# Seam order and a turned sample product in a two-layer mLSTM / Mamba-2 trunk

## The chip, the cores and the metric

One core of one Trainium2 chip. The metric is device time in microseconds of one execution of the whole program. Engines are named as the profile names them: PE is TensorE, DVE is VectorE, ACT is ScalarE, POOL is GpSimd; SP only issues the weight loads.

## What is computed

One inference step of a decoder trunk with two layers on 256 prompt tokens and 8 samples of 4 tokens each, 288 columns in all. Every layer does `x += mixer(rmsnorm(x))` and `x += convffn(rmsnorm(x))`. Layer 0 mixes with an mLSTM matrix memory, layer 1 with Mamba-2. The part of the Mamba-2 scan that matters here, for each group and head, with `h` the state:

```
cb    = C @ B^T                                   # scores of a group
wts   = cb * exp(-(acum_t - acum_s)) * dt
y     = wts @ x + (C @ h) * exp(acum)             # second term: the state's share
h_new = exp(acum_last) * h + sum(to_end * x * B)
g     = (y + D*x) * silu(z);  g *= rsqrt(mean(g*g) + eps)   # mean over a group of 512
```

For the prompt `h` starts at zero, so the second term exists for the 32 sample columns alone. The channel mixer is `(silu(conv(g)) * conv(v)) @ w_down`, with 2 x 5632 up-projected rows.

## The kernel before

**Layout.** Activations lie turned: features on the 128 partitions, the 288 tokens (`T`; 256 are `TP`, 32 are `TS`) along the free axis. Each matrix product is made in three passes of reduced precision: `w_hi*hi`, `w_hi*lo`, `w_lo*hi` (lines 395 to 397). Weights come in chunks of 128 output rows. For each chunk, in one fixed order through the whole program: SP loads `w_raw`, ACT rounds it to `w_hi` (L672), DVE subtracts to `w_lo` (L999), PE makes 48 products of 288 columns (33 in the down projection, where a chunk has 11 tiles of 128). There are two buffers of each weight tile. A chunk `c` may be split by ACT once PE is through chunk `c-2`. Results go round-robin through four PSUM banks, so PE may run three chunks ahead of DVE. Banks `M0` to `M3` belong to the mixers.

**Order of work.** All queues are written out by hand and in order; semaphores (`wait`, `until`) join them. The mLSTM heads and the Mamba groups are software-pipelined: while PE projects the ten chunks `j = 0..9` of group `u+1`, it does `b_mix(u, p, j)` behind chunk `j`. The steps of a group are: `j = 0` scores and transposes; odd `j` (1, 3, 5, 7) spread the decay rows of head pair `k` over the partitions; even `j` (2, 4, 6, 8) the products of pair `k`; `j = 9` the mean of squares. DVE and ACT do the same steps one place earlier in their loops, with conv and activation of the projected chunk (`b_post`) behind them. POOL holds the transfers of the states: `b_s` (updated and written back) and `b_sT` (the same state turned, only read), 512 KB each, and the weighting `b_xw` (L1651), which ACT and DVE split into `b_x` (L937, L938, L1405) before PE can use it.

**The state's share.** At even `j` PE multiplies the turned state of each of the 8 samples, as 128x128 weights, with 4 columns of `C` (16 instructions, `b_sT`), into `ps[:, M2, T:]`. The factor `exp(acum)` is spread over the partitions at odd `j` by two small products with `b_rsum`. DVE copies it (`b_ea`, L1389), multiplies (`b_yi`, L1412) and adds (L1415). POOL takes the decay of `b_s` from `b_ea` too.

**Seams.** Between stages PE waits for small serial work: the gate rows of either mixer (`gate_columns`, `gate_columns_b`, then `ga_low` / `gb_low`), the sum of squares in front of a channel mixer (`norm(k)` before the first up chunk), and the last `act_lo` between up and down projection. `out_part` opens an output projection with the newest group's tiles last in its order.

Of the kernel before, what the change touches and what calls it, by code (L numbers as in the profile page):

```python
# [25 lines left out]
F32 = mybir.dt.float32  # L26
F32R = mybir.dt.float32r
ACT = mybir.ActivationFunctionType
ALU = mybir.AluOpType
# [93 lines left out]

class Own:
# [17 lines left out]
def trunk(nc, d, o):  # L142

    with ExitStack() as ctx:
# [72 lines left out]
        with ExitStack() as st:  # L217
# [10 lines left out]
            b_yi = sb("b_yi", [P, TS], F32, st)  # L228
            b_rows = sb("b_rows", [64, 3, T], F32, st)
            b_nac2 = sb("b_nac2", [P, T], F32R, st)  # L230
            b_rsum = sb("b_rsum", [64, TS + 1], F32, st)
# [12 lines left out]
            b_ea = sb("b_ea", [P, TS], F32, st)  # L244

# [5 lines left out]
        b_tmp = b_xdt[0:64, 0:2, 0:T]  # L251
        b_th = work[:, :, :].rearrange("p a t -> p (a t)")[:, 0:BP]
# [46 lines left out]
            "b_wts", "b_xwr"))  # L299
        b_yst, b_decayed, b_sadd, b_spr, b_yg, b_gsq, b_gms, b_gvar, b_groot, b_gn, b_ghi, b_glo = map(sem, (  # L300
# [26 lines left out]
        def _(sp):  # L327
# [21 lines left out]
            def ffn(c0, up, down):  # L349
                with sp.Fori(0, 2) as h:  # L350
                    with sp.Fori(0, FH) as i:
                        for j in range(2):
                            load(Count(c0 + j, (h, C_FHALF), (i, 2)), up[h * (2 * FH) + i * 2 + j], CH)
                    with sp.Fori(0, KT) as i:
                        for j in range(2):
                            load(Count(c0 + 2 * FH + j, (h, C_FHALF), (i, 2)), down[h * (2 * KT) + i * 2 + j], DCH)
# [28 lines left out]
        def _(pe):  # L385
# [97 lines left out]
            def a_head(u, p, mixed):  # L483

                c = u.times(6)
                for j in range(6):
# [5 lines left out]
                    if mixed is not None:  # L492
                        a_mix(mixed, 1 - p, j)
# [10 lines left out]
            pe.wait_ge(ga_done, 1)  # L504
            pe.wait_ge(ga_low, 1)
# [28 lines left out]
            def ffn(layer, c0, n0, ea0, ed0, k):  # L534
                norm(k)
                with pe.Fori(0, 2) as h:
                    with pe.Fori(0, FH // 2) as i:
                        for j in range(4):
                            wait(pe, proj_taken, Count(ea0 + j - 3, (h, 2 * FH), (i, 4)))
                            if j == 0:  # L540

                                gemm(Count(c0 + j, (h, C_FHALF), (i, 4)), (n0 + j) % 4, hn_hi, hn_lo, range(KT),
                                     each=lambda t: wait(pe, hn_lo_ready, k * KT + t + 1))
                            else:
                                gemm(Count(c0 + j, (h, C_FHALF), (i, 4)), (n0 + j) % 4, hn_hi, hn_lo, range(KT))
                    wait(pe, f_alo, Count(layer * FT + FH // 2, (h, FH)))
                    pe.sem_inc(pe_passed, 1)
                    with pe.Fori(0, KT // 4) as i:
                        for j in range(4):
                            wait(pe, res_added, Count(ed0 + j - 3, (h, KT), (i, 4)))  # L550
                            for q in range(2):
                                if j == 0 and q == 1:
                                    wait(pe, f_alo, Count(layer * FT + FH, (h, FH)))
                                gemm(Count(c0 + 2 * FH + 2 * j + q, (h, C_FHALF), (i, 8)), (n0 + 2 * FH + j) % 4,
                                     act_hi, act_lo, range(q * FH // 2, (q + 1) * FH // 2), q == 0, q == 1)
# [6 lines left out]
            def gate_columns_b():  # L562
                pe.wait_ge(gb_rows, 1)
                for n, row in enumerate((0, 1, 2)):
                    for b in range(3):
                        w = P if b < 2 else TS
                        m = nc.tensor.transpose(ps[0:w, M1 if n < 2 else M2, 192 * (n % 2) + 64 * b:192 * (n % 2) + 64 * b + 64],
                                                b_rows[:, row, b * P:b * P + w], ident[0:64, 0:64])
                m.then_inc(gb_turned, 1)

            def b_mix(u, p, j):
                bT, cT = b_io[:, p, 0, :], b_io[:, p, 1, :]
                if j == 0:
                    wait(pe, b_silu, u.plus(1).times(6))
                    wait(pe, b_gvar, u)
                    wait(pe, b_sadd, u.times(8))
# [7 lines left out]
                if j in (1, 3, 5, 7):  # L584
# [11 lines left out]
                    mm(ps[:, M1, 0:T], b_sel[:, 1, :], b_nac2[:])  # L596
                    one_head = b_sel[0:64, :, :].bitcast(F32)
                    mm(ps[0:64, M1, T:T + TS], one_head[:, 0, 0:64], b_rsum[:, 0:TS])
                    mm(ps[64:P, M1, T:T + TS], one_head[:, 1, 0:64], b_rsum[:, 0:TS]).then_inc(b_rowsr, 1)
                if j in (2, 4, 6, 8):  # L600
                    k = (j - 2) // 2
                    ch = slice(k * P, (k + 1) * P)
# [3 lines left out]
                    wait(pe, b_sT_in, u.times(4).plus(k + 1).times(16))  # L606
                    for b in range(NB):
                        mm(ps[:, M2, T + SL * b:T + SL * (b + 1)], b_sT[:, b, :], cT[:, TP + SL * b:TP + SL * (b + 1)])
                    for e in range(2):
                        rows, hc = slice(64 * e, 64 * (e + 1)), slice(k * P + 64 * e, k * P + 64 * (e + 1))  # L610
                        mm(ps[rows, M2, 0:TP], b_xdt[:, 0, hc], b_dec[:, e, 0:TP], True, False)
                        mm(ps[rows, M2, P:TP], b_xdt[:, 1, hc], b_dec[:, e, TP:TP + P], False, False)
                        m = mm(ps[rows, M2, TP:T], b_xdt[0:TS, 2, hc], b_dec[0:TS, e, TP + P:SC], False, True)
                    m.then_inc(b_yst, 1)
# [7 lines left out]
                if j == 9:  # L622
                    wait(pe, b_gsq, u.plus(1).times(4))
                    wait(pe, b_yg, u.plus(1).times(4))
                    for k in range(4):
# [1205 lines left out]
```

## Time and profile before

| what | value |
|---|---|
| median of 3 runs | 3375.09 us (3370.61 to 3377.14) |
| the profiled execution's own time | 3377.63 us |
| its span, first to last instruction | 3376.0 us |
| PE busy | 3227.8 us, 96% |
| DVE busy | 2118.9 us, 63% |
| ACT busy | 1351.6 us, 40% |
| POOL busy | 888.1 us, 26% |
| mean granted PE clock | 0.965 |

A busy share is a mean over stages. A row's "idle before" is the time in which the engine did nothing in front of that instruction, with what ended it. PEclk is the mean granted clock of a stretch: 1.0 is 2.4 GHz, 0.5 is 1.2 GHz.

### The profile page before, as it was taken

The page shows a single profiled execution, that of the slowest core. Times are in us where ns is not written, and L with a number is a line of the kernel's source. Part 1 is how long each engine was busy: PE and PEld are TensorE (multiplying, and loading weights), DVE is VectorE, ACT ScalarE, POOL GpSimd, SP SyncE. Part 2 cuts the span into 40 slices and gives each one's busy share as a digit, 9 for nine tenths or more (in the row PEclk, how much of TensorE's full clock was granted, in tenths as well). Part 3 has the DMA queues.
Part 4 walks back from the last instruction along what each step waited for, and adds up shares of the span by engine and source line. Part 5 has one row for each costly group of instructions (what it writes and reads, how often), then busy time and mean ns, then how long its engine had stood idle before and what let it go on. Part 6 is the DMA issues. An engine that isn't in the chain of part 4 may idle for free.

```text
span 3376.0 us, 63895 instructions
## 1 busy us (share of the span) xinstructions
PE 3227.8 (96%) x23321; PEld 3141.6 (93%) x23321; DVE 2118.9 (63%) x3215; ACT 1351.6 (40%) x1694; POOL 888.1 (26%) x1123
## 2 busy tenths in 40 slices
PE   6999999999999999999999999999899999999997
PEld 6999999999999999988888888988799999999997
DVE  5555666666456765567775665676576764466744
ACT  4333334444334444443333333333245443344432
POOL 2110113222012321234541442443232220022221
PEclk9999999999999999999989888998899999999999
DMA  5354444444454444535544444444444444444444
GB/s 203 139 190 174 153 175 153 164 167 143 163 173 169 162 146 162 181 133 186 174 146 160 154 156 158 173 163 154 152 147 161 171 153 153 169 167 165 157 152 143
DMA packets 91383, 545.53 MB, mean 162 GB/s; under 512 B 11688, under 2 KB 12528, under 8 KB 43904
## 3 DMA queue, kind: packets, MB, share of 16 engines
q1 hardware_dynamic: 71872, 466.98, 39.3%
q0 software_dynamic: 19392, 76.98, 6.4%
q8 instruction: 73, 1.20, 0.1%
q14 instruction: 46, 0.38, 0.0%
HBM read 510.92 MB, written 32.99 MB: 161 GB/s over the span
## 4 chain that ended last, share of the span: by engine, by line
PE 79%; DVE 8%; issue 6%; ACT 4%; POOL 2%; DMA 1%; DVEq 0%; POOLq 0%; ACTq 0%; SPq 0%
PE ps L395 25%; PE ps L396 24%; PE ps L397 24%; PE ps L402 6%; ACT w_hi L672 2%; DVE w_lo L999 2%; DVE b_u L1348 1%; POOL sumsq L1506 1%; DVE b_u L1350 1%; DVE b_u L1346 1%; DVE work L1433 0%; DVE sumsq L1428 0%; DVE b_s L1422 0%; POOL b_xw L1651 0%; ACT b_out_hi L953 0%
## 5 line engine op out<-in xcount | busy, mean ns | idle before, releaser
L395 PE MATMUL ps<-hn_hi,w_hi 128*128 128x288 f32 x4896 | 1473.3, 301 | 40.3 <-DVE w_lo L999 17.4
L396 PE MATMUL ps<-hn_lo,w_hi 128*128 128x288 f32 x4896 | 1456.1, 297 | 0.0
L397 PE MATMUL ps<-hn_hi,w_lo 128*128 128x288 f32 x4896 | 1450.6, 296 | 0.0
L999 DVE TENSOR_TENSOR w_lo<-w_raw,w_hi 128x2048 fp32r<-128x2048 f32 (+1 forms) x482 | 1045.2, 2168 | 585.7 <-ACT w_hi L672 585.4
L672 ACT ACTIVATE w_hi<-w_raw 128x2048 fp32r<-128x2048 f32 (+1 forms) x482 | 858.0, 1780 | 1126.9 <-PE ps L397 1120.0
L395 PEld LDWEIGHTS ps<-hn_hi,w_hi 128*128 128x128 f32 x4896 | 930.2, 190 | 46.4 <-issue 24.8
L397 PEld LDWEIGHTS ps<-hn_hi,w_lo 128*128 128x128 f32 x4896 | 933.1, 191 | 0.0
L396 PEld LDWEIGHTS ps<-hn_lo,w_hi 128*128 128x128 f32 x4896 | 931.2, 190 | 1.2
L1583 POOL COPY f_new<-f_pad 128x2 f32 x176 | 242.7, 1379 | 1080.8 <-ACT f_u L847 1080.8
L395 PE MATMUL ps<-act_hi,w_hi 128*128 128x288 f32 x1408 | 416.7, 296 | 13.7 <-DVE act_lo L1278 13.7
L396 PE MATMUL ps<-act_lo,w_hi 128*128 128x288 f32 x1408 | 418.7, 297 | 0.0
L397 PE MATMUL ps<-act_hi,w_lo 128*128 128x288 f32 x1408 | 418.2, 297 | 0.0
L395 PEld LDWEIGHTS ps<-act_hi,w_hi 128*128 128x128 f32 x1408 | 267.9, 190 | 14.6 <-issue 14.6
L396 PEld LDWEIGHTS ps<-act_lo,w_hi 128*128 128x128 f32 x1408 | 267.8, 190 | 0.0
L397 PEld LDWEIGHTS ps<-act_hi,w_lo 128*128 128x128 f32 x1408 | 267.7, 190 | 0.0
L1506 POOL TENSOR_TENSOR sumsq<-sumsq,work 128x288 f32<-128x288 f32 x80 | 121.0, 1513 | 325.7 <-ACT work L687 303.9
L1620 POOL COPY b_new<-b_pad 128x3 f32<-128x3 f32 x48 | 116.6, 2430 | 315.2 <-ACT b_u L904 315.2
L395 PE MATMUL ps<-b_out_hi,w_hi 128*128 128x288 f32 x512 | 159.7, 312 | 23.0 <-DVE b_out_lo L1437 23.0
L850 ACT ACTIVATE act_hi<-f_act 128x288 f32 x88 | 39.1, 445 | 320.7 <-DVE f_act L1275 320.7
L396 PE MATMUL ps<-b_out_lo,w_hi 128*128 128x288 f32 x512 | 156.0, 305 | 0.0
L397 PE MATMUL ps<-b_out_hi,w_lo 128*128 128x288 f32 x512 | 155.7, 304 | 0.0
L395 PEld LDWEIGHTS ps<-b_out_hi,w_hi 128*128 128x128 f32 x512 | 100.9, 197 | 28.5 <-DVE b_out_lo L1437 28.1
(276 smaller groups left out, 3389.1 us busy)
## 6 DMA issues: line engine op xcount, KB each, us to landing
w_raw<-wf_up_in SPq DMA_DIRECT2D x176, 1024.0 KB, 4.8
w_raw<-wf_down_in SPq DMA_DIRECT2D x128, 704.0 KB, 4.0
w_raw<-wb_in_in SPq DMA_DIRECT2D x80, 1024.0 KB, 4.8
w_raw<-wa_in_in SPq DMA_DIRECT2D x48, 1024.0 KB, 5.0
w_raw<-wb_out_in SPq DMA_DIRECT2D x32, 1024.0 KB, 4.8
w_raw<-wa_out_in SPq DMA_DIRECT2D x16, 1024.0 KB, 4.8
b_sT<-b_sT_in POOLq DMA_DIRECT2D x32, 512.0 KB, 5.0
b_s<-b_s_in POOLq DMA_DIRECT2D x32, 512.0 KB, 3.9
```

What stands on the lines that cost most here:

```text
L395: nc.tensor.matmul(out, w_hi[:, s, col], hi[:, t, :], start=first and k == 0, stop=False)
L396: nc.tensor.matmul(out, w_hi[:, s, col], lo[:, t, :], start=False, stop=False)
L397: m = nc.tensor.matmul(out, w_lo[:, s, col], hi[:, t, :], start=False, stop=end)
L402: return nc.tensor.matmul(out, lhs, rhs, start=start, stop=stop, skip_group_check=True)
L672: A(w_hi[:, c.base % 2, 0:cols], w_raw[:, c.base % 2, 0:cols], ACT.Copy).then_inc(w_high, 1)
L850: A(act_hi[:, Count(par).add(i, 2).value, :], f_act[:, par, :], ACT.Copy).then_inc(f_ahi, 1)
L999: TT(w_lo[:, s, 0:cols], w_raw[:, s, 0:cols], w_hi[:, s, 0:cols].bitcast(F32), ALU.subtract).then_inc(w_low, 1)
L1346: STT(out, pad[:, 1:BP - 2], w(1), out, ALU.mult, ALU.add).then_inc(b_taps, 1)
L1348: STT(out, pad[:, 2:BP - 1], w(2), out, ALU.mult, ALU.add).then_inc(b_taps, 1)
L1506: G.tensor_tensor(sumsq[:], sumsq[:], work[:, buf, :], ALU.add).then_inc(sq_added, 1)
L1583: G.tensor_copy(f_new[:, n.value, 0:2], f_pad[:, s, TP:TP + 2])
L1620: G.tensor_copy(b_new[:, j, 0:3], b_pad[:, j % 2, TP:TP + 3])
```

## The change

Four edits of order and one of form, all on the one core:

1. **Gates.** PE's waits for `ga_done`, `ga_low` and for `gb_done`, `gb_low` move behind the first chunk of the second head or group. The gates of layer 1 get two more products, behind the new semaphores `gb_faded` and `gb_spread`.
2. **Channel mixer, start.** PE does the first up chunk tile by tile (`first_project`) and `norm(k)` behind it. ACT and DVE split the next chunk before their part of the norm. POOL loads `f_old` when the mixer is over, not after the norm.
3. **Up to down.** The first four down chunks are taken in the order `FIRST_DOWN`: first halves of two output tiles, then their second halves.
4. **State's share.** `C` of each sample, masked into 32 columns (`b_cm`), is the weight; the turned state streams past it (128 columns), at odd `j`, four samples side by side in four column groups of the array, into `ps[:, M3, P:2P]` (`b_yraw`). ACT takes it out scaled by `exp(acum)` (`b_ysr`), and one product with `fold` adds it to the head pair's sum. `b_ea`, `b_yi` and both adds go; the decay of `b_s` comes from a table `b_fade` made once.
5. **Around it.** The `b_dec` products alternate between the two 64-column halves. The mean of squares takes two products for four; POOL adds tiles 1 and 2 to tile 0 (`b_gsum`). POOL issues the next `b_sT` load at even `j`, in front of `b_xw`, as soon as `b_yraw` says that the buffer was read; before, it was at odd `j` behind the store of `b_s`.

```diff
+FIRST_DOWN = ((0, 0), (1, 0), (0, 1), (1, 1), (2, 0), (2, 1), (3, 0), (3, 1))
# PE, mLSTM: moved from in front of a_head(1) to behind its first chunk
+                        if j == 0 and u.base == 1:
+                            pe.wait_ge(ga_done, 1)
+                            pe.wait_ge(ga_low, 1)
# PE, channel mixer
-                norm(k)
+                        if first and j == 0:
+                            first_project(c, bank, k)
+                            norm(k)
...
+                    down_four(h, 0, FIRST_DOWN)
# PE, gate_columns_b
-                m.then_inc(gb_turned, 1)
+                pe.wait_ge(gb_faded, 1)
+                nc.tensor.transpose(ps[:, M2, 192:256], b_xdt[0:64, 0, 0:P], ident[0:64, 0:64])
+                pe.wait_ge(gb_spread, 1)
+                mm(ps[:, M3, :], mean_mat[0:64, :], b_spread).then_inc(gb_turned, 1)
# PE, b_mix, odd j
-                    mm(ps[0:64, M1, T:T + TS], one_head[:, 0, 0:64], b_rsum[:, 0:TS])
-                    mm(ps[64:P, M1, T:T + TS], one_head[:, 1, 0:64], b_rsum[:, 0:TS]).then_inc(b_rowsr, 1)
+                    wait(pe, b_cmr, u.plus(1))
+                    wait(pe, b_spr, u.times(4).plus(k))
+                    wait(pe, b_sT_in, u.times(4).plus(k + 1).times(16))
+                    for b in range(NB):
+                        g = b % 4
+                        m = mm(ps[TS * g:TS * (g + 1), M3, P:2 * P], b_cm_of[b], b_sT[:, b, :], b < 4, b >= 4)
+                    m.then_inc(b_yraw, 1)
# PE, b_mix, even j
-                    for b in range(NB):
-                        mm(ps[:, M2, T + SL * b:T + SL * (b + 1)], b_sT[:, b, :], cT[:, TP + SL * b:TP + SL * (b + 1)])
+                    wait(pe, b_ysr, u.times(4).plus(k + 1))
+                    for e, (rows, hc) in enumerate(halves):
                         mm(ps[rows, M2, 0:TP], b_xdt[:, 0, hc], b_dec[:, e, 0:TP], True, False)
+                    for e, (rows, hc) in enumerate(halves):
                         mm(ps[rows, M2, P:TP], b_xdt[:, 1, hc], b_dec[:, e, TP:TP + P], False, False)
...
+                    mm(ps[:, M2, TP:T], b_ys, fold[:], False, True).then_inc(b_yst, 1)
# PE, b_mix, j = 9
-                    for k in range(4):
-                        m = mm(ps[:, M2, 0:T], mean_mat[:], b_io[:, p, 2 + k, :], k == 0, k == 3)
+                    mm(ps[:, M2, 0:T], mean_mat[:], b_io[:, p, 2, :], True, False)
                     wait(pe, b_gsq, u.plus(1).times(4))
+                    mm(ps[:, M2, 0:T], mean_mat[:], b_io[:, p, 5, :], False, True).then_inc(b_gms, 1)
# ACT, b_mix, even j, in front of the exponential of b_dec
+                    wait(act, b_yraw, n.plus(1))
+                    for e in range(2):
+                        m = A(b_ys[:, 64 * e:64 * (e + 1)], ps[:, M3, P + 64 * e:P + 64 * (e + 1)], ACT.Copy, scale=b_eas[:, col])
+                    m.then_inc(b_ysr, 1)
# DVE
+                    V.tensor_copy(b_cm[:, :, 0:SL], packed(b_io[:, p, 1, :])).then_inc(b_cmr, 1)
-                    wait(dve, b_decayed, n)
-                    V.tensor_copy(b_ea[:], ps[:, M1, T:T + TS])
-                    b_link(u, 3 * k + 1, TT(b_yi[:], ps[:, M2, T:T + TS], b_ea[:], ALU.mult))
-                    b_link(u, 3 * k + 3, TT(y[:, TP:T], y[:, TP:T], b_yi[:], ALU.add))
+                    dve.wait_ge(gb_faded, 1)
+                    TT(b_spread..., head_ident..., b_ea4..., ALU.mult).then_inc(gb_spread, 1)
# POOL, even j, in front of b_xw
+                    if not (u.base == B_GROUPS - 1 and k == 3):
+                        until(b_yraw, n.plus(1))
+                        load_state(n.plus(1))
# POOL, odd j
-                        load_state(n.plus(1))
+                    if k in (1, 2):
+                        until(b_gsq, n.plus(1))
+                        G.tensor_tensor(b_io[:, p, 2, :], b_io[:, p, 2, :], b_io[:, p, 2 + k, :], ALU.add).then_inc(b_gsum, 1)
```

## Rows read from the trace of the kernel before

**Rows 1.** Waits of TensorE, whole kernel: microseconds in total, times, longest.
```profile
PE ps L402 <- DVE b_dec L1403: 28.3, 14, 5.8
...
PE ps L395 <- DVE act_lo L1278: 13.7, 4, 3.4
```

**Rows 2.** Timeline at the gates of the first mixer: start, length, engine, line, [idle before].
```profile
71.02 2.29 DVE L999 TENSOR_TENSOR w_lo<-w_raw,w_hi 128x2048 fp32r<-128x2048 f32 x1 [1.55 <-ACT w_hi L672]
...
80.76 0.58 PE L395 MATMUL ps<-hn_hi,w_hi 128*128 128x288 f32 x1 [4.99 <-issue]
```

**Rows 3.** Timeline in front of the first channel mixer.
```profile
532.79 2.29 DVE L999 TENSOR_TENSOR w_lo<-w_raw,w_hi 128x2048 fp32r<-128x2048 f32 x1 [1.01 <-ACT w_hi L672]
...
541.39 2.01 DVE L1014 SCALAR_TENSOR_TENSOR hn_lo<-x,norm_w,hn_hi  x2
...
543.14 1.33 PE L402 MATMUL ps<-sumsq,mean_mat 128*128 128x288 f32 x2 [5.94 <-POOL sumsq L1506]
```

**Rows 4.** Timeline between up and down projection, first half of layer 0.
```profile
830.19 2.29 DVE L999 TENSOR_TENSOR w_lo<-w_raw,w_hi 128x2048 fp32r<-128x2048 f32 x1 [1.34 <-ACT w_hi L672]
...
836.55 1.63 DVE L999 TENSOR_TENSOR w_lo<-w_raw,w_hi 128x1408 fp32r<-128x1408 f32 x1 [0.75 <-ACT w_hi L672]
...
835.97 0.40 PE L395 MATMUL ps<-act_hi,w_hi 128*128 128x288 f32 x1 [3.40 <-DVE act_lo L1278]
```

**Rows 5.** Timeline at the gates of the state-space mixer.
```profile
1482.84 0.45 DVE L1322 TENSOR_TENSOR b_nac<-b_rows,b_nac 64x288 fp32r<-64x288 f32 x1
...
1497.38 0.68 DVE L1375 TENSOR_TENSOR b_xdt<-ps,b_dtc 128x512 f32<-128x512 f32 x1
...
1483.39 0.58 PE L395 MATMUL ps<-hn_hi,w_hi 128*128 128x288 f32 x1 [4.80 <-issue]
```

**Rows 6.** Stretches: length, busy time and instructions by engine, PEclk, DMA.
```profile
836.00:842.00 6.00, 6.00 (x34) 6.00 (x35) 1.63 (x1) 0.52 (x1) 0.00 (x0) 0.72 0.40 124
1483.40:1492.00 8.60, 8.60 (x46) 8.60 (x47) 0.00 (x0) 0.00 (x0) 0.00 (x0) 0.68 0.33 121
1583.00:1793.00 210.00, 196.93 (x1338) 182.70 (x1337) 152.32 (x268) 80.92 (x119) 94.38 (x112) 0.92 0.47 162
```

**Rows 7.** TensorE blocks of a mixing step at full clock, and two forms like the new ones.
```profile
104.77 1.07 PE L402 MATMUL ps<-a_c,a_rows 128*32 128x256 f32 x16
...
1733.22 0.30 PE L402 MATMUL ps<-b_rsum,b_sel 64*64 64x32 f32 x4
...
1739.95 1.84 PE L402 MATMUL ps<-b_io,b_sT 128*128 128x4 f32 x16
1741.72 2.11 PE L402 MATMUL ps<-b_dec,b_xdt 128*64 128x256 f32 x12
```

**Rows 8.** Waits of VectorE in two mixing groups, 1583.3 to 1793.7 us.
```profile
DVE b_x L1405 <- ACT b_x L938: 17.8, 8, 3.5
DVE w_lo L999 <- ACT w_hi L672: 11.9, 12, 1.5
...
DVE b_io L1337 <- PE ps L397: 4.5, 3, 2.4
...
DVE b_pad L1334 <- PE ps L397: 1.6, 1, 1.6
```

**Rows 9.** Lines of VectorE and GpSimd: count, busy us, mean ns, idle before.
```profile
L1415 DVE TENSOR_TENSOR b_io<-b_io,b_yi 128x32 f32<-128x32 f32 x32 | 11.6, 362 | 1.1
...
L1412 DVE TENSOR_TENSOR b_yi<-ps,b_ea 128x32 f32<-128x32 f32 x32 | 5.8, 181 | 5.5 <-PE ps L402 5.4
...
L1506 POOL TENSOR_TENSOR sumsq<-sumsq,work 128x288 f32<-128x288 f32 x80 | 121.0, 1513 | 325.7 <-ACT work L687 303.9 <-ACT work L726 16.9 <-POOL sumsq L1506 2.9
...
L1601 POOL DMA_DIRECT2D b_sT<-b_sT_in x32 | 16.9, 529 | 1.8 <-issue 1.6
```

**Rows 10.** TensorE at the end of the last mixing group, half clock.
```profile
2418.89 3.57 PE L402 MATMUL ps<-b_io,b_sT 128*128 128x4 f32 x16 [5.76 <-DVE b_dec L1403]
...
2428.81 4.21 PE L402 MATMUL ps<-b_io,mean_mat 128*128 128x288 f32 x8 [0.70 <-ACT b_io L946]
```

More of the change, by code:

```diff
@@ L534, in ffn @@
             def ffn(layer, c0, n0, ea0, ed0, k):
-                norm(k)
[L536 to L546, printed above, removed]
-                    pe.sem_inc(pe_passed, 1)
[L548 to L555, printed above, removed]
@@ new lines, in up_four @@
+                def up_four(h, i, first=False):
+                    for j in range(4):
+                        wait(pe, proj_taken, Count(ea0 + j - 3).add(h, 2 * FH).add(i, 4))
+                        c, bank = Count(c0 + j).add(h, C_FHALF).add(i, 4), (n0 + j) % 4
+                        if first and j == 0:
+                            first_project(c, bank, k)
+                            norm(k)
+                        else:
+                            gemm(c, bank, hn_hi, hn_lo, range(KT))
@@ new lines, in down_four @@
+                def down_four(h, i, order):
+                    for n, (j, q) in enumerate(order):
+                        if q == 0:
+                            wait(pe, res_added, Count(ed0 + j - 3).add(h, KT).add(i, 4))
+                        elif order is FIRST_DOWN and j == 0:
+                            wait(pe, f_alo, Count(layer * FT + FH).add(h, FH))
+                        gemm(Count(c0 + 2 * FH + n).add(h, C_FHALF).add(i, 8), (n0 + 2 * FH + j) % 4,
+                             act_hi, act_lo, range(q * FH // 2, (q + 1) * FH // 2), q == 0, q == 1)
@@ new lines, in half @@
+                def half(h, done):
+                    with pe.Fori(0, FH // 2 - done) as i:
+                        up_four(h, i if done == 0 else i + done)
+                    wait(pe, f_alo, Count(layer * FT + FH // 2).add(h, FH))
+                    pe.sem_inc(pe_passed, 1)
+                    down_four(h, 0, FIRST_DOWN)
+                    with pe.Fori(0, KT // 4 - 1) as i:
+                        down_four(h, i + 1, DOWN)
+                up_four(0, 0, True)
+                half(0, 1)
@@ L575, in b_mix @@
                     wait(pe, b_gvar, u)
+                    wait(pe, b_ysr, u.times(4))
                     wait(pe, b_sadd, u.times(8))
@@ L837, in pair @@
                             split(c.plus(2))
+                            if first_pair and j == 0:
+                                norm(k)
                             if j == 1:
@@ L933, in b_mix @@
                     k = (j - 2) // 2
+                    n = u.times(4).plus(k)
+                    wait(act, b_yraw, n.plus(1))
+                    wait(act, b_yst, n.times(2))
+                    for e in range(2):
+                        head = n.times(2).plus(e).value
+                        col = slice(head, head + 1) if isinstance(head, int) else bass.ds(head, 1)
+                        m = A(b_ys[:, 64 * e:64 * (e + 1)], ps[:, M3, P + 64 * e:P + 64 * (e + 1)], ACT.Copy, scale=b_eas[:, col])
+                    m.then_inc(b_ysr, 1)
                     wait(act, b_dlog, u.times(4).plus(k + 1))
@@ L1250, in pair @@
                             c = Count(c0 + s).add(h, C_FHALF).add(i, 4)
+                            ahead = first_pair and j == 0
+                            if ahead:
+                                norm(k, lambda: split(c.plus(2)))
                             wait(dve, chunk_done, c.plus(1))
```

180 lines of the change are left out of this document (101 added, 79 removed).

## The prediction, made before the change was run

> **What bounds the kernel now.** I read the page first (PE is busy 96% of the span), then PE's waits, then the timelines around the long ones, then VectorE in the state-space groups. Two kinds of time can be had. One is PE's idle time at seams; each long gap costs again behind it, because the granted clock falls: in the stretch after the gap at 835.97, 33 products take 6.0 us at a clock of 0.72, and in the one at 1483.4, 46 take 8.6 us at 0.68 [rows 6]. At full clock the `b_rsum` block and a whole chunk of 48 fit between 1733.22 and 1739.95, 0.135 us a product [rows 7], so these would take 4.4 and 6.2 us: a gap of 3.4 to 5 us brings another 1.6 to 2.4 us of slow products. The other kind is work of PE inside the mixing groups. There PE shares the bound with VectorE: in two groups (210 us) VectorE is busy 152 us, and of its idle time only 4.5 + 1.6 us ended by PE's products directly; 17.8 us ended by ACT's `b_x`, which waits for GpSimd's `b_xw` [rows 6, 8]. VectorE works the queue take, decay rows, split, weights, `b_x`, conv, take, split, outputs, conv, and PE waits for it at `b_dec` 14 times, 28.3 us [rows 1].
>
> **Seams, one by one.**
>
> *Gates of layer 0.* PE stands 4.99 us until 80.76 [rows 2]. The next chunk's weights were split by 71.02 + 2.29 = 73.3, so its 48 products can start at once; they last 6.4 us, longer than the gate work that is left. The gap goes, and with it about 2.4 us of slow clock (by the second stretch of [rows 6], which follows a gap as long). Gain 7.4 us. Cover: if the gate work were over 6.4 us late, the rest would show in front of the mixing step.
>
> *Start of a channel mixer, twice.* PE stands until 543.14, 5.94 us, for the sum of squares; the first up chunk's weights were ready at 532.79 + 2.29 = 535.1 and the last `hn_lo` tile is written at 541.39 + 2.01 = 543.4 [rows 3]. With the chunk first, 14 tiles run under the wait, and the last two end about 0.4 us behind 543.4, at 543.9. Then comes the norm product, 0.4 to 0.7 us, and the second chunk starts near 544.4. Before, the first chunk began at 543.9 and, with the slow clock, ended near 551.9. Gain 7.5 us each, 15 us. What is late next is the norm itself: VectorE now splits a chunk between the sum and the reciprocal, so `rstd` comes near 550 and the first take with it. PE may run three chunks (19 us) ahead, so I cost this at nothing; without these banks it would cost 5 us. `f_old` is loaded some 60 us earlier on an idle GpSimd and delays nothing.
>
> *Up to down, four times.* PE stands 3.40 us until 835.97; all four together are 13.7 us [rows 1, 4]. With `FIRST_DOWN` the second chunk needs no `act_lo`, and its weights are ready at 830.19 + 2.29 = 832.5, just when PE is there. It ends at 836.9. The third chunk's weights are ready at 836.55 + 1.63 = 838.2 [rows 4]: this split sits behind `act_lo` on VectorE, so a gap of 1.3 us is left. Gain 3.7 - 1.35 = 2.35 us each, and 1.6 us more if the clock stays up [rows 6]; the bounds are 2.3 and 4.0, I take 3.25. 13 us.
>
> *Gates of layer 1.* PE's wait until 1483.39 ended with the low half of the decay rows, 1482.84 + 0.45 [rows 5]. This wait doesn't go: PE must now stand for `gb_spread`, which VectorE makes behind that very instruction: 512 elements a row, priced by the 0.68 us of [rows 5]. Then PE makes a product of 512 columns (the 288-column one of `mean_mat` is 4.21/4 = about 1 us at half clock [rows 10], so 0.8 to 1.8 us). The next chunk starts 1.5 to 2.5 us later than before. Loss 2 us, and 0.3 us for the new fill of `b_xdt` at the start of the stage.
>
> Seams together: 7.4 + 15 + 13 - 2.3 = 33 us.
>
> **The turned product on PE.** Out goes the block of 16 `b_sT` instructions, 1.77 us from its start to the next block's, and 0.30 us of `b_rsum` [rows 7]. In comes a block of the shape of the mLSTM's: 16 instructions in 1.07 us for 256 columns; 128 columns take half, to the same: 0.5 to 1.0 us, I take 0.5. The `fold` product has 32 columns, 0.25 us. The `b_dec` block lasts 2.1 us. Four instructions of 64-column groups with both halves together last only 0.30 us [rows 7], less than the length of two alone, so the alternating halves should overlap; the bounds are 1.0 us (full overlap) and 2.1 us (none). I take 1.0. Saved per head pair: 1.77 + 0.30 - 0.5 - 0.25 + 1.0 = 2.3 us, and two of four mean products, 0.9 us, per group.
>
> The Trainium skill (TensorEngine Tiling (Array Packing), Key Properties) says that tiles of the array run in parallel, but that a change of tiling mode drains TensorE. The new order changes the mode more often, at 32 places twice. No row here isolates a drain; the mLSTM's block contains two changes and still takes 1.07 us. By the page one would keep the overlap and add something per change; if that were 0.25 us a change, PE's saving would be 2.3 - 0.5 us, and the result would move by little, since the groups are bound as follows.
>
> **What of it reaches the end.** *Groups 1 to 7 of mixing.* Of VectorE's loop per group, 3 us are waits for PE itself and about half of the 11.9 us (two groups) for `w_hi`, which then ends 1.5 us behind PE's chunk [rows 8]: 3 + 3 = 6 us per group can go at most by a faster PE. VectorE's own work falls by `b_yi` 0.18, the add 0.36 [rows 9], the copy `b_ea` (as `b_yi`) and the chained waits, about 0.8 us a pair, 3.2 a group. Against it: GpSimd issues the state load (0.53 us, [rows 9]) in front of `b_xw`, and VectorE's `b_x` waits for that chain in every pair [rows 8], 2.1 us a group; and its two adds, 1.5 us each as L1506 [rows 9], delay `b_xw` of the last pair by 1 to 1.5 us. ACT's two new copies come before the exponential but under VectorE's split (2.3 us). `b_yraw` waits for the state transfer, issued a chunk pair (over 13 us) ahead and landing in 5 us: hidden. Net 6 + 3.2 - 2.1 - 1.3 = 5.8 us at most; since PE then idles more and its clock falls more often, I take 5. Bounds: 1 us (VectorE's loop unchanged) and PE's full 4 x 2.3 + 0.9 = 10 us. 7 x 5 = 35 us.
>
> *The last group* is mixed beside output chunks, with no conv work; VectorE waits for PE there. The first three pairs give 2.3 us each, with one of them at low clock 8 us. In the last, at half clock, nothing hides anything: 3.57 us of `b_sT` [rows 10] and half of `b_dec` go, 0.5 us of `fold` comes, 5 us; VectorE saves 0.6 us; of four mean products at 0.9 us three leave the chain, 2.7 us. 8 + 8.3 = 16 us.
>
> Mixer 51, seams 33, together 84 us. Against the profiled execution's own 3377.6 us that is 3294; this lies 2.5 us above the median of the runs, so 3291 us.
>
> **Rivals.**
> 1. *PE's saving reaches the end in full*: 7 x 10 + 17 + 33 = 120 us, 3255 us. For it: PE is 96% busy, and fewer slow stretches feed back. Against it: VectorE's loop above. 13%.
> 2. *VectorE binds the seven groups entirely and `b_dec` doesn't overlap*: 7 x 1 + 12, and seams at the low bound, 27: 46 us, 3329 us. For it: every `b_x` wait lies in VectorE's loop, and the load and the adds lengthen it. 15%.
> 3. *Slower: GpSimd's queue.* `until(b_yraw)` and the load now stand in front of `b_xw`; everything behind (`select`, the `b_s` load, decay) waits for PE's turned product, which waits for the former load. If this ring cost x us per pair more, 28 pairs decide: from x = 3 us it eats all 84. At x = 4 the time is 3375 - 84 + 112 = 3403 us. Against it: the product comes 1 us behind a chunk for which GpSimd's conv copy waits anyway. 3%.
> 4. *No change* by more than 0.2% (7 us): the seams' gain paid back by the groups. 3%.
>
> **Numbers.** Forecast as worked out, 3265 to 3320 us: 66%. The range that leaves out at most 2 in 10 runs from a little inside the first rival to the second: 3250 to 3332 us. A measurement of this kernel can tell about 0.2%, 7 us. Faster 0.94, same 0.03, slower 0.03.
>
> **What the profile after would show.** PE's waits of 5 to 6 us at 80, 537 and 2491 us gone; four waits of 1.3 us ended by `w_lo` where `act_lo` stood; a wait as long as before, for `gb_spread`, at the gates of layer 1. The `b_sT` block near 0.5 us at odd steps, `b_dec` near 1.0 at full clock; if it is 2.0, the halves don't overlap. In a group, VectorE's waits for PE nearly gone, its waits for `b_x` as long or longer, PE's waits for VectorE above the present 28 us, and a lower mean clock in spite of less work. If PE's waits in the groups don't grow, VectorE wasn't the bound and rival 1 holds; if `b_x` waits exceed 4 us a pair, rival 3.

## The result, and the profile of the changed kernel

The changed kernel takes 3313.73 us (median of four runs, 3311.35 to 3314.47) against 3374.93 us (3370.61 to 3377.14): a ratio of 0.9819, 95% interval 0.9807 to 0.9832, 61 us or 1.8% faster. The forecast was 3291 us with a range of 3250 to 3332: the direction and the range held, of the 84 us forecast 61 arrived. The profiled execution took 3311.35 us, span 3309.7.

TensorE's waits over the whole kernel (total, times, longest), which answer to [rows 1]:

```profile
PE ps L414 <- DVE b_x L1463: 40.4, 21, 3.4
PE ps L407 <- DVE b_out_lo L1493: 29.6, 16, 6.7
PE ps L414 <- DVE b_dec L1461: 24.3, 16, 5.1
PE ps L407 <- DVE w_lo L1047: 21.5, 10, 6.7
PE ps L414 <- DVE b_s L1478: 18.1, 16, 2.4
```

The waits for `act_lo` and, but for 2.1 us, for the sum of squares are gone. The wait for VectorE's `b_x` is new, and that for `b_s` grew from 5.3 us in the kernel before:

```profile
PE ps L402 <- DVE b_s L1422: 5.3, 6, 2.4
```

The timeline at the seams (start, length, what it is, idle before): the third down chunk, for [rows 4]; then the gates of layer 1, for [rows 5].

```profile
822.36 0.37 PE L407 MATMUL ps<-act_hi,w_hi 128*128 128x288 f32 x1 [1.11 <-DVE w_lo L1047]
...
1462.84 2.07 PE L414 MATMUL ps<-b_xdt,mean_mat 64*128 64x512 f32 x2 [5.55 <-DVE b_xdt L1380]
1464.85 0.61 PE L407 MATMUL ps<-hn_hi,w_hi 128*128 128x288 f32 x1
```

The TensorE blocks of a mixing step at full clock, for [rows 7]: read a block's length from its start to the next one's start.

```profile
1752.63 0.65 PE L414 MATMUL ps<-b_sT,b_rows 128*32 128x128 f32 x16
...
1759.79 0.96 PE L414 MATMUL ps<-b_dec,b_xdt 128*64 128x256 f32 x12
1760.67 0.41 PE L414 MATMUL ps<-fold,b_rows 128*128 128x32 f32 x2
1760.92 0.71 PE L414 MATMUL ps<-b_bm,b_x 96*128 96x512 f32 x2
```

So `b_sT` takes 0.58 us to the next chunk's first product (1.77 before), `b_dec` 0.88 (2.04), `fold` 0.25; the forecasts were 0.5, 1.0 and 0.25, and `b_dec` came out a little below its lower bound of 1.0. Yet the two groups last 208 us where they lasted 210. The stretch (length, busy time of PE, PE's weight loads, DVE, ACT and POOL with instructions, clock, DMA) for [rows 6], and VectorE's waits in it for [rows 8]:

```profile
1561.00:1769.00 208.00, 177.72 (x1316) 166.52 (x1315) 150.25 (x247) 83.93 (x135) 93.80 (x117) 0.92 0.48 167
```

```profile
DVE b_x L1463 <- ACT b_x L986: 22.5, 8, 4.4
DVE w_lo L1047 <- ACT w_hi L702: 12.1, 12, 1.5
DVE b_io L1411 <- ACT work L958: 9.1, 12, 1.9
DVE b_s L1478 <- POOL b_s L1726: 4.5, 2, 2.5
```

TensorE is busy 19 us less there and the groups end 2 us sooner: the rest became idle time. In these groups VectorE no longer waits for TensorE. Its waits for `b_x` grew by 4.7 us and for `b_s` by 2.3.

**Where the time went, by landmarks.** The starts of the same products in both timelines give the gain of each stretch in the two spans (66.3 us):

| stretch | forecast | measured |
|---|---|---|
| gates of layer 0 | 7.4 | 7.6 |
| first channel mixer, start | 7.5 | 8.4 |
| up to down, four places | 13 | 14.6 (3.5, 3.1, 4.6, 3.5) |
| gates of layer 1, to the next chunk | -2.3 | -4.0 |
| mixing groups 1 to 7, with the output parts between | 35 | 18.8 |
| last group | 16 | 16.3 |
| second channel mixer, start | 7.5 | 4.6 |

### The profile page after: what moved, and what is told of

It is laid out like the page before. It is cut to its first block, busy times and chain, and to the rows that moved or that the text cites. A ratio compares the mean times of both kernels' runs of the same rounds, so it can differ in the third digit from the quotient of the medians.

```text
span 3309.7 us, 63483 instructions
## 1 busy us (share of the span) xinstructions
PE 3126.7 (94%) x23228; PEld 3056.7 (92%) x23228; DVE 2109.6 (64%) x3130; ACT 1337.5 (40%) x1741; POOL 908.0 (27%) x1139
## 4 chain that ended last, share of the span: by engine, by line
PE 74%; DVE 7%; issue 6%; ACT 4%; POOL 4%; DMA 3%; DVEq 0%; POOLq 0%; ACTq 0%; SPq 0%
PE ps L407 24%; PE ps L409 23%; PE ps L408 23%; PE ps L414 3%; ACT w_hi L702 2%; DMA b_s<-b_s_in 2%; POOL b_s L1726 1%; POOL b_xw L1715 1%; DVE b_u L1407 1%; DVE w_lo L1047 1%; DVE b_s L1478 1%; DVE b_u L1409 1%; DVE b_u L1405 1%; POOL b_new L1681 0%; DVE work L1489 0%
## 5 line engine op out<-in xcount | busy, mean ns | idle before, releaser
L1047 DVE TENSOR_TENSOR w_lo<-w_raw,w_hi 128x2048 fp32r<-128x2048 f32 (+1 forms) x482 | 1027.8, 2132 | 567.9 <-ACT w_hi L702 567.9
L1681 POOL COPY b_new<-b_pad 128x3 f32<-128x3 f32 x48 | 102.1, 2128 | 295.7 <-ACT b_u L944 295.7
L882 ACT ACTIVATE act_hi<-f_act 128x288 f32 (+1 forms) x88 | 39.2, 446 | 317.4 <-DVE f_act L1327 317.4
L1726 POOL TENSOR_TENSOR b_s<-b_s,b_fade 128x1024 f32<-128x1024 f32 x32 | 90.6, 2830 | 161.3 <-DMA b_s<-b_s_in 151.0
```

The costliest lines, as they stand in the source:

```text
L882: A(act_hi[:, Count(par).add(i, 2).value, :], f_act[:, par, :], ACT.Copy).then_inc(f_ahi, 1)
L1047: TT(w_lo[:, s, 0:cols], w_raw[:, s, 0:cols], w_hi[:, s, 0:cols].bitcast(F32), ALU.subtract).then_inc(w_low, 1)
L1681: G.tensor_copy(b_new[:, j, 0:3], b_pad[:, j % 2, TP:TP + 3])
L1726: G.tensor_tensor(b_s[:], b_s[:], dec, ALU.mult).then_inc(b_decayed, 1)
```

## The experiments

Twelve kernels, each timed over several rounds against the kernel before. Times are medians; the kernel before lay at 3373.8 to 3376.6 us in these comparisons. Kernels of different comparisons are set against each other by their medians, so a difference of 3 us or less between two of them says nothing.

**1. The seam edits alone, and the mixer edits alone.** Each is the kernel before with one part of the diff.

> The kernel before with the seam edits alone (order at the two gate seams, start of both channel mixers, up to down projection, the early result of the fold); the mixer of layer 1 is untouched. My theory: the seams and the mixer add up. In the two profiled spans the seams gave 7.6 (gates, layer 0), 8.4 (first channel mixer), 14.6 (four up-to-down places) and 4.6 us before the second channel mixer; there the second wait for the output product had grown, so 4.6 to 7.5 us; the gates of layer 1, without the spread product behind them, should gain as those of layer 0 did, 5 to 7 us. Sum 40 to 45 us: about 3331 us, ratio 0.986 to 0.989. Rival: the seams only hand their gain on to the mixer of layer 1, which gives it back as VectorE and the loads get later: under 30 us, above 3345 us.

> The kernel before with the mixer edits alone (turned product, halves side by side, the fold, GpSimd's two sums ahead of the mean, the spread product of the gates, the load ahead of GpSimd's weighting); all seams as before. My theory: groups 1 to 7 give what VectorE lets through (about 20 us in the two spans, 2 to 5 each), the last group 16 us, less the spread product's 4 us: 30 to 36 us, about 3342 us, ratio 0.989 to 0.991. My prediction's own terms gave 51 us (3324 us). If seams and mixer together give less or more than the 61 us between the two medians, the difference is what the two parts take from one another; additive within 5 us is what I expect.

Measured: seams 3331.6 us, ratio 0.9866 (0.9849 to 0.9882), 45 us; mixer 3353.1 us, ratio 0.9930 (0.9912 to 0.9948), 24 us. The seams did what was expected. The mixer edits gave 6 us less than the lowest that I expected, and less than half of the 51 us of the prediction: the shortfall lies in the mixer. The two sum to 68.5 us and the change gives 61.2, 7 us less, where I had expected them to add within 5. That is not clear of the intervals, but the traces show a place for most of it. From the norm of layer 1 to the end of group 1's mixing the span is 176.7 us in the kernel before, 169.0 with the seams, 178.8 with the mixer, 177.3 with both: 6.2 us are lost in combination. The seam edit removes TensorE's wait at the gates, and the spread product, a mixer edit, puts one back in the same place.

**2. The two halves by turns, undone.**

```diff
                     for e, (rows, hc) in enumerate(halves):
                         mm(ps[rows, M2, 0:TP], b_xdt[:, 0, hc], b_dec[:, e, 0:TP], True, False)
-                    for e, (rows, hc) in enumerate(halves):
                         mm(ps[rows, M2, P:TP], b_xdt[:, 1, hc], b_dec[:, e, TP:TP + P], False, False)
-                    for e, (rows, hc) in enumerate(halves):
                         mm(ps[rows, M2, TP:T], b_xdt[:, 2, hc], b_dec[:, e, TP + P:SC], False, False)
```

> The changed kernel with the six products of the state output issued half after half (three products on columns 0 to 63, then three on columns 64 to 127) and not by turns. The old kernel's block of this kind took 2.1 us, the changed one's 0.9 us, so I expect 0.9 to 1.2 us more of TensorE for each of the 32 blocks, 29 to 38 us in all. Theory A (VectorE binds groups 1 to 7): TensorE there idles for VectorE's rows anyway, the added time goes into those gaps, and only the last group's four blocks and part of another reach the end: 4 to 10 us, about 3320 us. Theory B (TensorE still binds in the groups, and the gain was lost elsewhere): 29 us or more, 3343 us and above. If the time does not rise at all, the block's gain did not come from the turns but from the shape.

Measured: 3314.9 us, 1.2 us more than the changed kernel, which is no difference. The timeline of this kernel:

```profile
1760.30 1.44 PE L414 MATMUL ps<-b_dec,b_xdt 128*64 128x256 f32 x12
1761.67 0.41 PE L414 MATMUL ps<-fold,b_rows 128*128 128x32 f32 x2
```

The block takes 1.37 us against 0.88, so 32 of them cost TensorE about 15 us (I had expected 29 to 38), and almost nothing of it reaches the end, less than the 4 to 10 us of theory A. In the traces this kernel is 2.3 us behind after seven mixing groups and 5.1 after the last; then TensorE waits 1.96 us for `b_out_lo` where the changed kernel waits 6.05, which gives 4 us back. TensorE doesn't bind groups 1 to 7. The order of the old kernel was also half after half, at 2.04 us. The edit leaves one difference to it: the third product now takes all 128 rows (`b_xdt[:, 2, hc]`), where the old one took 32 (`b_xdt[0:TS, 2, hc]`, a tile of 32 by 64). That form, not the alternation, gave 0.67 of the 1.16 us.

**3. GpSimd's weighting ahead of its copies.** `b_xw` is made (`b_weigh`: its waits and its three products, moved whole) before the copies of `b_new` for the next group, not behind them and the load.

```diff
                 for j in range(10):
+                    if mixed is not None and j < 9:
+                        b_weigh(mixed, j + 1)
                     b_post(u, p, j)
```

> The changed kernel with GpSimd's weighting of the x rows (1.1 us, read by TensorE's state product) issued ahead of its copies for the next group, and not behind them and the loads. Theory A (the chain GpSimd copy, weighting, TensorE, ScalarE, VectorE's wait for the turned rows is what holds the loop; that wait is 22.5 us in 8 places over two groups): the wait shrinks by the copies' time of up to 2 us at 28 places, 20 to 55 us less, 3260 to 3295 us. Theory B (VectorE binds by its own work and by what its waits hide in one another): the wait for the rows shrinks and another, for the load or for GpSimd's product, grows in its place: within 8 us of the changed kernel.

Measured: 3296.1 us, 17.6 us less than the changed kernel. That is just below the 20 to 55 us of theory A and well above the 8 of B. Over groups 2 and 3 VectorE's wait for `b_x` fell from 22.5 to 5.3 us, and its wait for `b_s` rose from 4.5 to 12.6:

```profile
DVE b_s L1478 <- POOL b_s L1718: 12.6, 5, 4.1
...
DVE b_x L1463 <- ACT b_x L986: 5.3, 4, 1.7
```

So the chain through GpSimd was in the loop, with a second one close behind it. Part of what made the first one so long is seen in the changed kernel's timeline at one pair of group 3 (its longest such wait); GpSimd first, then VectorE:

```profile
1733.71 3.27 POOL L1681 COPY b_new<-b_pad 128x3 f32<-128x3 f32 x1 [2.85 <-ACT b_u L944]
1736.92 0.20 POOL L1682 COPY b_new<-b_pad 128x24 f32<-128x24 f32 x1
1737.07 0.54 POOL L1686 DMA_DIRECT2D b_old<-b_old_in  x1
1737.98 0.54 POOL L1688 DMA_DIRECT2D bconv_out<-b_new  x1 [0.38 <-issue]
1738.93 0.54 POOL L1662 DMA_DIRECT2D b_sT<-b_sT_in  x1 [0.41 <-issue]
1739.56 1.11 POOL L1715 TENSOR_TENSOR b_xw<-b_xdt,b_end 128x128 f32<-128x128 f32 x3
```

```profile
1733.72 2.27 DVE L1047 TENSOR_TENSOR w_lo<-w_raw,w_hi 128x2048 fp32r<-128x2048 f32 x1
1735.92 1.01 DVE L1461 TENSOR_TENSOR b_dec<-b_dec,b_cb 128x832 f32<-128x832 f32 x1
1741.36 0.28 DVE L1463 TENSOR_TENSOR b_x<-b_xw,b_x 32x128 fp32r<-32x128 f32 x1 [4.43 <-ACT b_x L986]
```

The copy of three columns takes 3.27 us, the one of 24 columns behind it 0.20: it ends as VectorE's split and weights end (1736.93). Only then do the loads and the weighting run, then ScalarE's part of the split of `b_x`, and VectorE stands for 4.43 us. The split and the chain run one after the other; the prediction had no term for this. The same copy takes 3.26 to 3.87 us at the first three pairs of both groups. At the fourth pair, which has no copy, the weighting itself takes 3.15 and 3.42 us. The kernel before shows it too:

```profile
1712.25 3.97 POOL L1620 COPY b_new<-b_pad 128x3 f32<-128x3 f32 x1 [5.39 <-ACT b_u L904]
```

The Trainium skill (SBUF — State Buffer, SBUF: two separate sides) says that GpSimd and a VectorE instruction with two SBUF inputs share a port pair as an exclusive lock, held for the whole instruction; by that rule the copy waits inside its own span, and the trace agrees. It also shows that the copy did not get in between two such instructions of VectorE that follow each other at once.

**4. The load of the turned state behind the weighting; and without GpSimd's sums.** The first moves one issue behind the weighting and the copy of the next heads' picks (`select`); the second also drops `b_gsum` and gives TensorE its four mean products back.

```diff
-                    if not (u.base == B_GROUPS - 1 and k == 3):
-                        until(b_yraw, n.plus(1))
-                        load_state(n.plus(1))
...
                     m.then_inc(b_xwr, 1)
                     if k < 3:
                         select(k + 1)
+                    if not (u.base == B_GROUPS - 1 and k == 3):
+                        until(b_yraw, n.plus(1))
+                        load_state(n.plus(1))
```

> The changed kernel with GpSimd's issue of the turned state's load behind its weighting of the x rows and its copy of the heads' picks (still behind the product that read the buffer). The issue takes 0.54 to 0.58 us on GpSimd; in front of the weighting it stands between the copies and TensorE's state product. Theory A (GpSimd's chain up to the weighting holds the loop, as weighting ahead of the copies gave 17.6 us): each of 28 places gains up to 0.6 us, less where the turned state then comes too late (it takes 5.9 us from issue to landing and has over 10 us): 5 to 15 us less, 3299 to 3309 us. Theory B (the place of the issue is hidden): within 4 us of the changed kernel's 3314. That the load behind comes late and makes the next block wait: above 3318 us, with a wait for the load on TensorE.

> As the kernel before it in this list (load issued behind weighting and picks), and also without GpSimd's two sums for the mean: TensorE takes four products of 288 columns for it, as in the kernel before. GpSimd loses 1.6 us a group, TensorE gets two products of 288 columns more, about 1 us a group. Theory A (GpSimd's queue is in the loop): 3 to 8 us less than with the load moved alone, in groups 1 to 7; the last group pays about 1 us. Theory B (the sums run where GpSimd waits for its load anyway): equal to the load moved alone within 3 us, or 1 to 3 us above it.

Measured: 3296.0 us with the load moved (one of its four executions took 3305.4), 3295.9 us with the sums gone too. The place of one issue of 0.54 us, 28 times in groups 1 to 7 (15 us), is worth 17.7 us, above the 5 to 15 that I expected and about what it would be if each issue stood in the serial chain in full. VectorE's wait for `b_x` over two groups is 18.5 us in this kernel, near the 17.8 of [rows 8]. But GpSimd's fades (the products that decay `b_s` by `b_fade`) also got shorter, 74.8 us for all 32 against 90.6, which points at fewer meetings with VectorE's work; how much of the 17.7 us is the issue itself and how much such shifts isn't separated. Sums on GpSimd or two more products on TensorE: no difference. The prediction's 1.3 us a group for the sums, 9 us in all, doesn't show, unless the two products cost as much.

**5. The load of the batch state ahead as well.** On top of experiment 3, `b_s` is loaded right behind the weighting.

```diff
                 m.then_inc(b_xwr, 1)
+                until(b_s_out, n.times(16))
+                pool.dma_start(b_s[:], d["b_s"][n.value]).then_inc(b_s_in, 16)
```

> The kernel with the weighting ahead of the copies, and now also the load of the batch state (4 KB in each of 128 rows, 6.3 us from issue to landing) issued right behind the weighting, ahead of the copies for the next group. With the weighting ahead, VectorE's wait for the turned rows fell from 22.5 to 5.3 us over groups 2 and 3, but its wait for GpSimd's faded state rose from 4.5 to 12.6 us, and GpSimd waited 48 us for that load. Theory A (this single-buffered load, fade and add are the next chain in the loop): its 12.6 us of two groups go, the issue comes 4 to 8 us earlier in every second column and 0 to 1 us in the others: 4 to 5 us a group in seven groups, 25 to 35 us less, 3261 to 3271 us. Theory B (VectorE's own work or TensorE now binds): under 8 us less than 3296 us. Worse is possible if waiting for the store of the state before (3.6 us to landing) holds up the copies: above 3298 us.

Measured: 3255.0 us, 41 us less than experiment 3, more than the 25 to 35 that I expected, and 59 us less than the changed kernel (ratio to the kernel before 0.9646, 0.9629 to 0.9662). VectorE's waits for `b_s` over groups 2 and 3 fell to 1.9 us. Across layer 1's mixing, GpSimd's fade of `b_s` starts behind a much shorter wait for its load (count, busy, mean ns, idle before; the changed kernel, experiment 3, then this one):

```profile
L1726 POOL TENSOR_TENSOR b_s<-b_s,b_fade 128x1024 f32<-128x1024 f32 x32 | 90.6, 2830 | 161.3 <-DMA b_s<-b_s_in 151.0 <-ACT b_u L944 10.2
...
L1718 POOL TENSOR_TENSOR b_s<-b_s,b_fade 128x1024 f32<-128x1024 f32 x32 | 63.0, 1969 | 188.7 <-DMA b_s<-b_s_in 188.7
...
L1715 POOL TENSOR_TENSOR b_s<-b_s,b_fade 128x1024 f32<-128x1024 f32 x32 | 68.5, 2142 | 71.4 <-DMA b_s<-b_s_in 67.2 <-ACT b_u L944 4.2
```

The fades themselves got shorter by experiment 3's order, not by this one (1969 ns, then 2142); what this load's place brings is the wait. The ring store, load, fade, add of the single buffer was the second chain.

**6. The same order on the old mixer.** The seam edits and the old mixer, with weighting and load ahead.

> The kernel with the seam edits alone (mixer as in the kernel before, 3331.6 us) and GpSimd's weighting and the load of the batch state ahead of its copies, as in the kernel that took 3255 us with the turned mixer. It says what the mixer's edits are worth when GpSimd's order no longer holds the loop. Theory A (the mixer edits had their full value of 35 us and more in TensorE, and GpSimd's order hid it; the old mixer kept TensorE busy 197 of 210 us in groups 2 and 3, so the new order can win it only what is left): 10 to 25 us less than 3331.6, so 3307 to 3322 us, and the mixer edits are worth 52 to 67 us on this order against 18 on the old one. Theory B (the order is worth as much with either mixer, 55 to 59 us): 3273 to 3277 us, and the mixer edits are worth about 20 us on either.

Measured: 3313.0 us, 18.6 us less than the seams alone. VectorE's waits in groups 2 and 3 show the old mixer near TensorE's bound: now the wait for TensorE is the largest.

```profile
DVE b_io L1365 <- PE ps L403: 13.9, 5, 6.1
...
DVE b_x L1433 <- ACT b_x L959: 2.9, 3, 1.0
```

This settles where the gain went. On GpSimd's old order the mixer edits are worth 17.9 us (3331.6 to 3313.7); on the new order 58 us (3313.0 to 3255.0). The blocks cost TensorE what the prediction said, and GpSimd's queue held back most of what that was worth.

**7. The halves apart, on the new order.**

> The kernel of 3255 us (weighting and load ahead) with the six products of the state output half after half, which costs TensorE 0.48 us at each of 32 blocks, 15 us in all (1.37 against 0.89 us a block in the profiles); with GpSimd's old order this cost 1.2 us of the 15. Theory A (TensorE is now nearer to the bound, busy 173 of 192 us in groups 2 and 3): 4 to 12 us more, 3259 to 3267 us. Theory B (VectorE, busy 155 of 192 with short waits, binds alone): 0 to 3 us more.

Measured: 3261.3 us, 6.3 us more than experiment 5. Of the same 15 us of TensorE, 1 reached the end on the old order and 6 do now. Part of that contrast is the wait of 4 us that experiment 2 got back; up to the end of the seventh mixing group the two traces show 2.3 us there and 5.2 here.

**8. The gates of layer 1 later.** TensorE turns the gate rows and makes the spread product behind the first chunk of group 1.

```diff
                         if j == 0 and u.base == 1:
+                            gate_columns_b()
                             pe.wait_ge(gb_done, 1)
...
-                    elif j == 9:
-                        gate_columns_b()
```

> The changed kernel with TensorE's turn of the layer-1 gate rows and the spread product issued behind the first chunk of group 1 and not in front of it. In front, TensorE waits 5.5 us for VectorE's spread and works 2 us at the lower clock. My theory: the wait goes, as the chunk of some 6.4 us covers it, and the product runs at the full clock; behind it TensorE waits for ScalarE's copies out of the banks (2 us) before it may mix: 4 to 6 us less, about 3309 us. Rival: the wait only moves to the copies of ScalarE and to VectorE's chunk behind them, less than 2 us gained.

Measured: 3304.7 us, 9.1 us less, above my 4 to 6. The wait of 5.55 us is gone; the two product instructions take 0.6 us each where they took 1.1; TensorE then waits 1.9 us for ScalarE's copies.

**9. Together.** Experiments 3, 5 and 8 with the turned state's load also behind the picks (experiment 4's first edit), and then without that last edit:

> The kernel of 3255 us (weighting and the load of the batch state ahead of the copies), with the gates of layer 1 behind the first chunk (9 us alone) and the load of the turned state behind the picks. If the gains add: 3255 less 9, and 0 to 4 for the load, 3242 to 3247 us. If the load of the turned state is late now that its queue carries the other load first (it has to land before the next block, some 21 us later), TensorE waits for it: 3250 us or more.

> The kernel of 3255.0 us (weighting and the load of the batch state ahead of the copies) with the gates of layer 1 behind the first chunk alone; the load of the turned state stays ahead of the picks. With that load behind the picks as well it was 3263.9 us. The landmarks of that run show group 1 ending where it ended without the late gates (1554.0 against 1553.8 us), so the late gates gained nothing there, and groups 5 to 6 and the last group longer by 3.1 and 4.5 us. If the place of the turned state's load made these losses: 3250 to 3256 us here. If the late gates made them (by shifting the loads): 3261 us or more.

Measured: 3263.9 us with the load behind, 3248.5 us without (0.9623 of the kernel before, 0.9607 to 0.9639). This is the fastest kernel of the study, 65 us below the change. The same edit that gained 17.7 us in experiment 4 lost 15.4 us here; I had expected 0 to 4 us of gain, or that TensorE would wait for the load, and the trace shows no such wait. Already at the first weighting of group 1 the two diverge, first the fast kernel, then the slow one:

```profile
1479.06 1.10 POOL L1737 TENSOR_TENSOR b_xw<-b_xdt,b_end 128x128 f32<-128x128 f32 x3 [3.51 <-DVE b_xdt L1440]
1480.11 0.57 POOL L1742 DMA_DIRECT2D b_s<-b_s_in  x1
```

```profile
1478.55 4.93 POOL L1737 TENSOR_TENSOR b_xw<-b_xdt,b_end 128x128 f32<-128x128 f32 x3 [3.08 <-DVE b_xdt L1440]
1483.44 0.57 POOL L1742 DMA_DIRECT2D b_s<-b_s_in  x1
```

The weighting starts 0.5 us earlier in the slow kernel, lasts 3.8 us longer, and the load behind it is 3.3 us late; group 1 ends 5.1 us later. VectorE's split runs from 1480.52 us in the fast kernel, behind the weighting, and from 1480.02 in the slow one, in which the weighting ends only when split and weights have ended (1483.23). But this first difference doesn't explain the loss. In the kernel of experiment 5 the same weighting also takes 4.93 us, and its group 1 lasts 93.6 us from one `b_xdt` of VectorE to the next group's, as in the fast kernel (93.5), against 98.8 in the slow one:

```profile
1483.54 4.93 POOL L1738 TENSOR_TENSOR b_xw<-b_xdt,b_end 128x128 f32<-128x128 f32 x3 [3.07 <-DVE b_xdt L1441]
```

The slow kernel falls behind at the third pair. There a product of VectorE's convolution takes 2.98 us, from the time of GpSimd's copy of the picks to the end of its fade; in experiment 5 the same product takes 0.56. First experiment 5, then the slow kernel:

```profile
1529.16 0.56 DVE L1409 SCALAR_TENSOR_TENSOR b_u<-b_pad,b_conv,b_u 128x312 f32<-128x312 f32 x1
...
1536.95 0.53 PE L414 MATMUL ps<-b_nac,b_sel 128*128 128x288 f32 x2 [0.57 <-DVE b_s L1478]
```

```profile
1524.13 0.54 POOL L1694 CAST b_sel<-head_ident 128x256 fp32r<-128x256 f32 x1
...
1525.17 1.91 POOL L1714 TENSOR_TENSOR b_s<-b_s,b_fade 128x1024 f32<-128x1024 f32 x1
1524.45 2.98 DVE L1408 SCALAR_TENSOR_TENSOR b_u<-b_pad,b_conv,b_u 128x312 f32<-128x312 f32 x1
...
1534.23 0.85 PE L414 MATMUL ps<-b_nac,b_sel 128*128 128x288 f32 x2 [2.59 <-DVE b_s L1477]
```

TensorE then waits 2.59 us for `b_s` instead of 0.57, and from 1534 to 1545 us its granted clock is 0.69, where experiment 5 has 1.0 from 1537 to 1545. Over the whole kernel TensorE waits 34.7 us for `b_s` in the slow kernel and 26.7 in the fast one. The only difference between the two programs is the place of the load; that it works through such meetings is shown for group 1 alone, and where the other 10 us go stays open. My reading that the late gates gained nothing fell: they are worth 6.6 us here as well (3255.0 to 3248.5).

## Why the prediction came out as it did

**Right.** The four TensorE forms (0.58, 0.88, 0.25 us, and two mean products for four); the gates of layer 0; the first channel mixer's start; the gap of 1.1 us that stays between up and down, forecast at 1.3; the last group, where VectorE had no convolution work and 16 us of 16 arrived; and that TensorE would idle in the groups. The time fell inside the range because the range went down to 1 us a group in the mixing groups, not because the 5 us forecast for them held.

**The step that failed: "What of it reaches the end", groups 1 to 7, 5 us each.** It measured 18.8 us in seven groups in place of 35, 16 of the 18 us that the sum missed in the spans. Its parts:

- "about half of the 11.9 us for `w_hi`" would go: they stayed, 12.1 us. With the order changed they still lay at 10.0 to 12.9 us.
- VectorE's own work fell only from 152.3 to 150.3 us in two groups, 1.0 a group where 3.2 were booked. The three small instructions gave 3.4 a group, as priced. Most of what took it back is VectorE's product with `silu(z)`, 8 times in two groups: 3.7 us before, 8.3 after. Some of them now run beside GpSimd's fades (1.61 us in place of 0.46 at 1704.38 us), and all 32 fades grew from 68.9 to 90.6 us. The splits did not grow: 50.8 and 49.1 us.

```profile
L1417 DVE TENSOR_TENSOR b_io<-b_io 128x288 f32<-128x288 f32 x8 | 3.7, 459 | 0.3
...
L1473 DVE TENSOR_TENSOR b_io<-b_io 128x288 f32<-128x288 f32 x8 | 8.3, 1034 | 0.3
```

- "GpSimd issues the state load in front of `b_xw`, 2.1 us a group": its place measured 17.7 us in seven groups, 2.5 each, with the shifts of experiment 4 in it. The sign and nearly the size were right.
- The adds, 1.3 us a group, made no difference against the two products that they replace.
- Not priced at all: that the copies, the load and the weighting start only when VectorE's split and weights are over, though the kernel before already shows it. The prediction knew the wait (`b_x`, 17.8 us) but took it for a fixed share of VectorE's loop, where it was the end of a GpSimd chain that could be taken out. Rival 1, the full saving of TensorE, is where the mixer edits move once that chain is gone (58 us measured, 87 in the rival, 51 in my sum).

**Smaller misses.** The gates of layer 1 cost 4.0 us to the next chunk, not 2.3: the product of 512 columns took 2.0 us at half clock, above my bounds. The second channel mixer's start gave 4.6 us, not 7.5: TensorE came to the last output rows earlier than VectorE had them ready, and its wait for `b_out_lo` there rose from 2.25 to 6.05 us. The 3.7 us in the sum for up to down doesn't follow from its rows, which give 3.4 (13.7 us in four places); the 3.25 us taken were nearly right. The other 5 us between 3291 and 3314 are the reference: the profiled execution lay 2.5 us above the median before and 2.4 below it after.

**Drains.** The prediction left out of its sum the rule of the Trainium skill (TensorEngine Tiling (Array Packing), Key Properties) that a change of tiling mode drains TensorE, as no row isolated one. Experiment 2 comes nearest: with the third product in the rows of its neighbours the block fell from 2.04 to 1.37 us. The trace agrees with the rule here, but the product's row count changed with the mode, so the two are not separated.

## What to carry to other kernels

Price a faster block by the queue that must keep up with it: take the loop of the engine that will bind next, and ask of each of its waits whether it is fixed or the end of a chain in another engine's queue. A DMA issue of half a microsecond in front of a small operation may cost its full time at each repetition, but the sign is not fixed: the same move gained 17.7 us on one order and lost 15.4 on another, so time such an edit again after every other reorder. Starting the single-buffered ring (store, load, use, add) as early as its queue allowed was worth 41 us here. Test a disputed saving on both sides of the suspected bound: the same edits were worth 18 us before the reorder and 58 us behind it.

## What the runs showed of the hardware

- A GpSimd copy of 3 columns took 3.27 us beside two-input work of VectorE, and 0.20 us was enough for 24 columns without it; three small products took 1.10 or 4.93 us, by half a microsecond of phase. It also goes the other way: beside GpSimd's copy of the picks and its fade, a VectorE instruction of 0.56 us took 2.98. Whether such a stretch costs anything depends on who waits: the 4.93 us cost nothing that shows in experiment 5, the 2.98 us were followed by 5 us of loss in experiment 9.
- Six products of the state output on 64-column halves took 2.04 us with a third product of 32 rows, 1.37 us with all of 128 rows, and 0.88 us when the halves also alternate.
- Sixteen instructions that stream 128 columns of the state past 32-column groups took 0.58 us; the same work with the state as 128x128 weights took 1.77 us.
